# Two norms at the seam of two blocks made one, column tiles alternated, pooling and weight loads reordered

## The reference, cut to what matters

```
h = concatenate([meta_tokens, x], axis=1)
for l in range(2):
    u = rms_norm(h, norm_w[l]) @ w_in[l]
    f_in, f_gate, p_in, p_gate, c_q, c_kv, k_r, a_gate = split(u)
    y_f = fourier_mix(f_in, fourier_w[l])        # DFT over tokens and over 64 channels
    y_p = pool_mix(p_in, pool_w[l], pool_scale)  # window means over 2, 4, 8, 16 tokens
    y_a = mla_mix(c_q, c_kv, k_r, ...)
    h = h + concatenate([y_f * silu(f_gate), y_p * silu(p_gate), y_a * silu(a_gate)]) @ w_out[l]
return rms_norm(h, final_norm_w)[:, 16:]
```

## Time and profile before

| | us |
|---|---|
| median of 3 runs | 4046.81 (4042.68 to 4050.09) |
| the profiled execution | 4042.67 |
| its span | 4040.9 |
| mean granted clock of TensorE | 0.964 of 2.4 GHz |

### The profile page before, as it was taken

The page is one execution under the profiler, slowest core; times in us unless marked ns, Lnnn a source line. Parts: engine busy times, 40 slices in busy tenths (PEclk is TensorE's granted clock), DMA queues, the critical chain, the costliest instruction groups (busy, mean ns, idle before and its releaser), DMA issues.

```text
span 4040.9 us, 51127 instructions
## 1 busy us (share of the span) xinstructions
PE 3743.9 (93%) x20820; PEld 3311.2 (82%) x20820; DVE 1718.9 (43%) x3136; ACT 1265.5 (31%) x2868; POOL 1091.6 (27%) x806
## 2 busy tenths in 40 slices
PE   6999998999999899999899999968988998898898
PEld 5787777888887788777778888858988998898898
DVE  6624554433325552455443332554334334333333
ACT  3212443034331211244313333122245422134541
POOL 2533222321113362322231221326310023530002
PEclk9999999999999999999999999979989999998999
DMA  3111110401114212111130112322100031110012
GB/s 113 37 68 63 35 50 32 147 31 42 42 40 176 87 42 78 47 40 44 42 141 29 42 40 79 130 83 65 43 26 19 20 108 56 60 52 13 14 41 95
DMA packets 85195, 243.91 MB, mean 60 GB/s; under 512 B 10720, under 2 KB 25312, under 8 KB 84960
## 3 DMA queue, kind: packets, MB, share of 16 engines
q1 hardware_dynamic: 84960, 240.64, 17.4%
HBM read 190.07 MB, written 50.53 MB: 60 GB/s over the span
## 4 chain that ended last, share of the span: by engine, by line
PE 70%; DVE 14%; ACT 7%; issue 5%; DMA 2%; POOL 2%; SPq 1%; DVEq 0%; POOLq 0%; ACTq 0%
PE pj L1212 27%; PE pS L1212 21%; PE po L1420 4%; PE po L1311 4%; PE pS L1400 3%; PE pS L1402 2%; DVE tmp L2030 1%; PE pS L1282 1%; DVE KK L2042 1%; PE pS L1283 1%; PE pt L1298 1%; DVE tmp L2033 1%; ACT PT L1612 1%; PE pj L1386 1%; DVE tmp L2027 1%
## 5 line engine op out<-in xcount | busy, mean ns | idle before, releaser
L2471 POOL TENSOR_SCALAR Whi<-stage 128x1024 fp32r<-128x1024 f32 (+4 forms) x272 | 277.8, 1021 | 2138.9 <-DMA stage<-wstream 1328.4
L1212 PE MATMUL pj<-Hhi,Whi 128*128 128x512 f32 x1648 | 657.5, 399 | 8.3 <-DVE Hlo L1901 3.3
L1212 PE MATMUL pj<-Hhi,Wlo 128*128 128x512 f32 x1648 | 645.5, 392 | 0.0
L1212 PE MATMUL pj<-Hlo,Whi 128*128 128x512 f32 x1648 | 645.0, 391 | 0.0
L2473 POOL TENSOR_TENSOR Wlo<-stage,Whi 128x1024 fp32r<-128x1024 f32 (+4 forms) x272 | 621.9, 2287 | 22.7
L1212 PEld LDWEIGHTS pj<-Hhi,Whi 128*128 128x128 f32 x1648 | 311.6, 189 | 76.3 <-ACT PT L1612 6.6
L1212 PEld LDWEIGHTS pj<-Hhi,Wlo 128*128 128x128 f32 x1648 | 311.0, 189 | 66.8
L1212 PEld LDWEIGHTS pj<-Hlo,Whi 128*128 128x128 f32 x1648 | 311.6, 189 | 61.4
L1212 PE MATMUL pS<-Hhi,Whi 128*128 128x512 f32 x784 | 312.7, 399 | 12.2 <-DVE Hlo L1901 5.1
L1212 PE MATMUL pS<-Hlo,Whi 128*128 128x512 f32 x784 | 310.0, 395 | 0.0
L1212 PE MATMUL pS<-Hhi,Wlo 128*128 128x512 f32 x784 | 309.5, 395 | 0.0
(11 more groups left out here) (389 smaller groups left out, 7735.8 us busy)
## 6 DMA issues: line engine op xcount, KB each, us to landing
stage<-wstream SPq DMA_DIRECT2D x228, 512.0 KB, 4.3
merged<-Mb SPq DMA_DIRECT2D x32, 512.0 KB, 2.9
Mb<-merged SPq DMA_DIRECT2D x32, 512.0 KB, 5.1
gates<-tmp SPq DMA_DIRECT2D x48, 256.0 KB, 2.2
TH<-gates SPq DMA_DIRECT2D x24, 512.0 KB, 6.1
xres<-X SPq DMA_DIRECT2D x16, 520.0 KB, 5.7
xr<-xres SPq DMA_DIRECT2D x16, 520.0 KB, 4.6
X<-xT SPq DMA_DIRECT2D x16, 256.0 KB, 6.8
```

What stands on the lines that cost most here:

```text
L1212: x = pe.e.matmul(ps, w[a][:, v.koff + k * P:v.koff + k * P + P], moving(v.of, b, k, v.t0, v.n), start=k == 0 and i == 0, stop=k == v.K - ...
L2471: pool.e.tensor_scalar(upper, stage, 1.0, 0.0, ALU.mult, ALU.add).then_inc(*pool.tick("whi", c))
```

## The change

1. **The seam.** While the last projections of block 1 run, ACT also squares x times final_g (`square` of kind "g", into accg) and DVE adds those. With s = sum(x^2) and g = sum((x final_g)^2), the two norms in one are x final_g norm_w / sqrt(g/D + EPS (s/D + EPS)): `last_sums` makes that per half of the tokens, with the meta tokens' squares in one more column. `row_spread` spreads it, `norm2` scales X directly with the product of the two gains (vec 98 to 105, and vec 60 to 67 for the 16 meta tokens). `between` is gone. The residual needs X by the first norm still: `scaled` does this on DVE behind `amix` in layer 0, and `scaled_out` stores it behind the DFT. The meta tokens and the rope tables come at the start of the last `output1` (`tables2_in`).
2. **Column tiles.** In both layers f0, f1 and p0 alternate by k in all three column tiles, and the norm of tile c + 1 stands in the order ahead of the group of tile c. `phase()` and `small_in` move behind the three groups.
3. **Weight loads.** Load c stands at the unit behind the last use of weight c - 3.
4. **Split by ACT.** For five of the eight DFT pieces ACT makes the upper half and POOL the lower one only.
5. **Pooling.** `pool0` moves behind the DFT, the window sums of `pool1` (`pool1_sums`) directly behind it, and the rest of `pool1` between the gates of p0 and those of f1. The order of the gates is f0, p0, f1, p1, and was f0, f1, p0, p1.
6. Tiles get other addresses in SBUF, and `ones` shrinks to 8 columns.

```diff
-        loaded = 0
-        for u, upto in self.upto:
-            last = min(upto, len(self.weights) - 1)
-            u["loads"] = range(loaded, last + 1)
-            loaded = max(loaded, last + 1)
+        at = 0
+        for c in range(len(self.weights)):
+            at = max(at, self.first[c].id if c < NR else self.used_at[c - NR] + 1)
+            self.units[at].setdefault("loads", []).append(c)
...
     def between(self, sums):
-        ph = self.phase()
-        rs = self.spread(sums) + self.spread(self.rstd("1", [self.accs[1]], D, 1))
-        u = self.put("between", rs=[("rs", x.id) for x in rs], x_ready=self.x_ready[0] + self.x_ready[1])
-        self.accs = {0: ("accs", u.id)}
-        self.phase()
-        u = self.put("between_out", of=u.id)
+        power = ("power", sums.id, 0)
+        self.rs = [self.row_spread("RS2", 0, [(24, META)] + [(20 + i, P) for i in range(3)], power)]
...
     def fourier_pool(self, l, norm):
+        f = [self.in2("f_copy", key("f", i), x=i, box={}, emptied="f_copy") for i in range(2)]
+        p = [self.in2("p_copy", key("p", i), x=i, box={}, emptied="p_copy") for i in range(2)]
+        for c in range(3):
+            if c < 2:
+                norm(c + 1)
+            self.together([f[0][c], f[1][c], p[0][c]], {} if c else self.inside)
+        f_ready = [("f_copy", f[i][2].id) for i in range(2)]
+        self.phase()
...
         self.put("small_in", l=l)
-        self.together([f[0][0], f[1][0], p[0][0]], self.inside)
-        for c in (1, 2):
-            self.run([f[0][c], f[1][c], p[0][c]])
         u = self.put("gmix", l=l, po_free=self.po_free)
...
-        u = self.put("pool0", l=l, p_ready=p_ready[0], folded=("lo", fold, 5), a_ready=a_ready)
-        z_ready = [("lo", u.id, 1)]
+        if l == 0:
+            self.put("scaled", rs=("rs", row[1].id))
+            lv_free = ("final1", 7)
...
+        if l == 0:
+            self.put("scaled_out")
+        u = self.put("pool0", l=l, p_ready=p_ready[0], folded=("lo", fold, 5), lv_free=lv_free, a_ready=a_ready)
+        z_ready = [("lo", u.id, 1)]
+        levels = self.put("pool1_sums", l=l, p_ready=p_ready[1], z_ready=z_ready)
...
-        for i in range(2):
+        def gate_f(i):
             self.run(self.in2("gate_f", key("fg", i), x=i, box={}, sets=slot, emptied="silu2", fy_ready=fy_ready[i], ph3=ph3,
                               y_free=self.y_free, l=l))
...
+        gate_f(0)
         gate_p(0, z_ready)
-        u = self.put("pool1", l=l, p_ready=p_ready[1], z_ready=z_ready, z_free=z_free[0], a_ready=a_ready)
+        u = self.put("pool1", l=l, levels=levels.id, z_free=z_free[0], a_ready=a_ready)
+        gate_f(1)
         gate_p(1, [("lo", u.id, 1)])
...
+def by_act(key):
+    return key[0] == "dft" and key[1:] not in ((0, 0, 0), (0, 0, 1), (1, 0, 0))
...
+    def last_sums(u):        # TensorE
+        for i, acc in enumerate((m.acc, m.accg)):
+            for j in range(4):
+                t0, col = 512 * u.c + j * P, 16 * u.c + 4 * i + j
+                x = pe.e.matmul(m.po[:, col:col + 1], acc[:, t0:t0 + P], ones[:, 0:1], start=True, stop=True)
+        if u.c == 0:
+            pe.wait_ge(("meta_square", u.meta))
+            for k in range(8):
+                x = pe.e.matmul(m.po[0:META, 8:9], m.sqm[:, k, :], ones[:, 0:1], start=k == 0, stop=k == 7)
...
+    def split(c):            # ACT, at the unit that carries load c
+        act.wait_ge(("w_in", c))
+        act.wait_ge(("wused", c - NR))
+        act.e.activation(m.W[c % NR][0][:, 0:n], m.stage[c % NS][:, 0:n], ACT.Copy).then_inc(*act.tick("whi_act", c))
...
+    def pool1_sums(u):       # POOL
         pool.wait_ge(u.p_ready)
         for x in u.z_ready:
             pool.wait_ge(x)
```

More of the change, by code:

```diff
@@ L189, in memory @@
[L189 to L195, removed]
@@ L328, in add @@
         if u.opens:
-            u.box["c"] = self.weight(u, u.key, u.ahead)
+            u.box["c"] = self.weight(u.key)
         if u.box is not None:
             u["c"] = u.box["c"]
+            if u.ends:
+                self.used_at[u.c] = u.id
         if u.banked:
@@ L798, in output1 @@
                     if i == 0:
-                        sums = self.rstd("1", [self.accs[0]], D, 0, within=True)
+                        sums = self.last_sums(0, meta.id) if last else self.rstd("1", [self.accs[0]], D, 0, within=True)
                     else:
-                        u["inside"] = {3: [sums]}
+                        u["inside"] = {4 if last else 3: [sums]}
             ring_free[e % 2] = ("residual", u.id)
@@ L877, in fourier_pool @@
         self.run(p[1])
+        row = self.scaled(self.half_sums, fold) if l == 0 else []
         p_ready = [("p_copy", p[i][2].id) for i in range(2)]
@@ L1241, in spread, with row_spread @@
         x.then_inc(*pe.tick("spread", u.id))
+    def row_spread(u):
+        pe.wait_ge(u.powers)
+        pe.wait_ge(u.free)
+        o = 0
+        for col, n in u.cols:
+            x = pe.e.matmul(m.pj[u.bank][:, o:o + n], m.st[0:n, col:col + 1].to_broadcast([n, P]), ident[0:n, 0:n],
+                            start=True, stop=True)
+            o += n
+        x.then_inc(*pe.tick("row_spread", u.id))
+    def last_sums(u):
+        for x in u.accs:
+            pe.wait_ge(x)
+        pe.wait_ge(u.po_free)
+        for i, acc in enumerate((m.acc, m.accg)):
[6 more added lines that the diff above has]
+                x = pe.e.matmul(m.po[0:META, 8:9], m.sqm[:, k, :], ones[:, 0:1], start=k == 0, stop=k == 7)
+        x.then_inc(*pe.tick("last_sums", u.id))
     def ln(u):
@@ L1469, in square, with meta_squares, row_spread @@
         dst = acc[:, u.t0:u.t0 + u.n] if u.k == 0 else sq[u.slot][:, 0:u.n]
-        act.e.activation(dst, src, ACT.Square).then_inc(*act.tick("square", u.id))
+        if u.of == "g":
+            act.e.activation(dst, src, ACT.Square, scale=m.vec[:, 52 + u.k:53 + u.k]).then_inc(*act.tick("square", u.id))
+        else:
+            act.e.activation(dst, src, ACT.Square).then_inc(*act.tick("square", u.id))
+    def meta_squares(u):
+        for k in range(8):
+            act.wait_ge(("meta_in", k))
+        phase_met(u)
+        act.e.activation(m.sqm[:, :, :], m.X[:, :, 0:META], ACT.Square).then_inc(*act.tick("meta_square", u.id))
+    def row_spread(u):
+        n = sum(x for _, x in u.cols)
+        act.wait_ge(("row_spread", u.id))
+        act.wait_ge(u.freed)
+        phase_met(u)
+        act.e.activation((m.RS2 if u.dst == "RS2" else m.RSy)[:, u.t0:u.t0 + n], m.pj[u.bank][:, 0:n], ACT.Copy).then_inc(
+            *act.tick("rs", u.id))
     def spread(u):
@@ L1839, in scalar_program @@
     for u in order.units:
+        for c in u.loads or ():
+            if by_act(order.weights[c]):
+                split(c)
         if u.kind in parts:
@@ L2470, in load @@
         pool.wait_ge(("wused", c - NR))
-        pool.e.tensor_scalar(upper, stage, 1.0, 0.0, ALU.mult, ALU.add).then_inc(*pool.tick("whi", c))
-        pool.wait_ge(("whi", c))
+        if by_act(order.weights[c]):
+            pool.wait_ge(("whi_act", c))
+        else:
+            pool.e.tensor_scalar(upper, stage, 1.0, 0.0, ALU.mult, ALU.add).then_inc(*pool.tick("whi", c))
+            pool.wait_ge(("whi", c))
         TT(lower, stage, upper.bitcast(F32), ALU.subtract).then_inc(*pool.tick("wlo", c))
@@ L2566, in pool1 @@
         level(u, 3, m.lv[1], m.lv[0], 4, 4, 8, 1048)
-    parts = {"phase": phase, "sums": sums, "norm": norm, "mix_in": mix_in, "ln": ln, "values": values, "between": between,
-             "proj": proj, "small_in": small_in, "pool0": pool0, "pool1": pool1}
+    parts = {"phase": phase, "sums": sums, "last_sums": last_sums, "norm": norm, "mix_in": mix_in, "ln": ln, "values": values,
+             "proj": proj, "small_in": small_in, "pool0": pool0, "pool1_sums": pool1_sums}
     for u in order.units:
```

241 lines of the change are left out of this document (136 added, 105 removed).

## The result

The changed kernel takes **4126.6 us** (median of 4 runs, 4117.4 to 4128.6), the kernel before in the same runs 4045.8: a ratio of 1.0195, with a 95% interval of 1.0177 to 1.0212. It is 1.95% slower. I had forecast 4037 and a range of 4005 to 4061. The profiled execution took 4128.6 (span 4126.6), so it is compared with the one before of 4042.7.

The account below looks back on a forecast made before the run. TensorE, busy 93% of the span, was taken as the bound, so only its gaps and slow clock counted. Terms -40 + 31 - 12 - 3.5 + 11.5 + 3 = -10 took the median 4046.8 to 4037 us, range 4005 to 4061.

Parts of the forecast that it names:

- part 6: Attention a: splits now ahead of a step's power delay it, mostly covered; +3 us, bounds 0 to +36.
- Rival (c): Attention a: ACT stands behind each delayed power, so the next step's copies and exponentials come late; +31, 4068 us; chance 0.17.
- The seam: Between the blocks: one norm for two and an earlier third weight shorten TensorE's waits; -40 us, bounds -32 to -43.
- The small inputs: Before gmix in both layers: TensorE waits for small transfers issued behind POOL's splits; +31 us, bounds 0 to +36.
- Loads one slot later: Layer starts and layer 1's copy stall: two third-weight waits and the stall vanish; -12 us, bounds -6 to -14.
- DFT: ACT's five upper halves delay odd copies but ready later weights: layer 0 +1 us, layer 1 -4.5.
- the 14.2 us by the rule on the two engines: Layer 0's DFT: scalings plus all lower halves, if DVE and POOL lock each other out; sum 1.5 us higher.
- Pooling: Both layers: POOL's levels delay the first Fy product, so TensorE waits for gate banks; +11.5 us, bounds -15 to +20.
- (a): Before gmix: the small inputs don't hold TensorE, so part of +31 shrinks to nothing; 4006 us; chance 0.18.
- (b): Pooling: POOL clears its levels before TensorE's banks fill, so its term becomes -15; 4011 us; chance 0.12.
- (d): Between the blocks: the seam yields only 30, with a late third weight and longer slow clock; 4047 us; chance 0.08.
- The row behind the prediction: Profile row of DVE scalings: two grew by 2.2 us beside one 3.4 us POOL add, agreeing with the lock in kind.

Follow-up runs that it names:

- e4: Changed kernel with only a weight's transfer issued earlier, ahead of the gate store; POOL still splits before the power: 4088.6 us, ratio 1.0105.
- e8: Changed kernel with POOL's powers put ahead of loads, plus square buffers alternating in order of making, as before: 4058.9 us, ratio 1.0030.
- e2: Kernel before with only the weight-load rule changed, to one slot after the last use of the weight three back: 4129.5 us, ratio 1.0206.
- e1: Changed kernel with the old rule for weight loads, weight c loaded when weight c-2 is opened: 4048.1 us, ratio 1.0004.
- c3: c1 with the loads in the last merge of each layer of block 1 back on the old rule: 4028.3 us, ratio 0.9975.
- e5: Changed kernel with POOL's powers ahead of loads, plus POOL's mark before its splits and small inputs issued before the third transfer: 4047.4 us, ratio 1.0006.
- e7: Changed kernel with POOL's powers ahead of loads, plus pool1_sums behind the first three gate_f tiles: 4057.5 us, ratio 1.0031.
- d1: c3 with the seventh DFT piece's split back on POOL and the seam's last two squares behind the norm's first two slices: 4026.4 us, ratio 0.9954.
- c1: Changed kernel with four edits together: powers before loads, small inputs first, pool1_sums later, square buffers alternating: 4034.4 us, ratio 0.9982.

## Why the prediction was wrong

**The step that failed is part 6.** It reads: "a 3.6 us split delays the power by 1.8 us. The next use of its result is at 413.15, 5 us after it is ready, so it is mostly covered", +3, bounds 0 to +36. It measured +64. Two things in it were wrong. First, I let the split start "as the filler ends". A split starts when its weight has landed, and the request stands right behind the weight's last use, on SP behind the gate store: it lands 5 us after that. At five loads of layer 0 POOL waited for a transfer, 54.7 us in all, with a power queued behind four of them. In the kernel before the transfer of the load shown was as late (issued at 423.35, landed 4.9 us later) and harmless, since POOL did the power first:

```profile
424.53 0.55 POOL L2514 TENSOR_TENSOR st<-st,vec 128x1 f32<-128x1 f32 x1 [8.33 <-DVE st L2173]
...
428.33 1.06 POOL L2471 TENSOR_SCALAR Whi<-stage 128x1024 fp32r<-128x1024 f32 x1 [2.98 <-DMA stage<-wstream]
```

That is the 38 us of e4. Second, the cover. I took 5 us of slack from one step early in a head and gave it to all. Ten steps of each layer had a split ahead of the power, 20 and not 40 in all; e4 gives 26 us for them by the splits alone. Rival (c) had named place and mechanism and its +31 is near that part, but it too left the transfer out. It had a chance of 0.17.

**Left out altogether:** the diff changes a buffer index for the squares, and I gave it no term. In the first sums the squares of one half of x share one buffer, so ACT and DVE take turns, 1.45 us a square: the first sums start 4.4 us earlier in e8. The rest of the 9.3 us at the start goes with the load rule: at 340 us e2, with the rule and the old index, is 2.7 us behind the kernel before, and e1, with the old rule and the new index, 5.4. In the rest of block 2 the rule and the index make 8.8 us more, of which e1 leaves 1.1. In the rest of block 1 the ends of the two merges lose 3.9 and 3.4 us, where a split now falls beside DVE's last work; c3 shortens TensorE's waits there from 4.6 to 2.2 and 2.3.

**The seam, -32.9 for -40.** The mechanism was right. Two terms were small. In times of before (after, less the delay of 74.1) the projection ends at 2650.4 and not at 2648.5, since the sums for both norms take 2.3 us and the granted clock behind them is 0.60 until the projection ends, and one addition behind it took 2.75 us for 0.69; and the nine tiles took 42.5 us at a granted clock of 0.87 where I had 38.8: slow clock cost 5.5, not 3.

**The small inputs, +30.6 for +31,** by the chain as told: three splits for POOL (7.3 us), then 4.5 us from first issue to first use. e5 undoes it and confirms the cause.

**Loads one slot later, -8.8 for -12.** The copy stall in layer 1 is gone as told (-5.3). The two waits for a third weight are gone too, but the wait for the norm ahead of each grew: from 3.3 to 5.4 us at the start of block 1's layer 1 and from 2.7 to 4.8 in block 2's. So they gave 2.9 and 0.6 us, forecast 4.5 and 2.5.

**DFT, +0.2 for -3.5.** ACT's odd copies come 3.2 us later (5.5 for 2.3 in layer 1), not 1.8: the gain at the weight behind is spent. In layer 0 the eight scalings took 13.3 us, forecast 13. The +1 for layer 0 doesn't follow from its own terms either: 1.8 + 0.7 - 2.6 is about nothing, before any slow clock. And the 14.2 us by the rule on the two engines are 1.2 above 13, not 1.5.

**Pooling, +10.4 for +11.5,** by the queue on POOL that I named; in e7, where the queue is gone, so is the wait of 7.0 us, though shorter waits take most of its place.

So rivals (a), (b) and (d) didn't happen, though the seam came near (d). All parts but attention a and the two without a term make +4 together (forecast: -13); those three make 82.

## What to carry to other kernels

When a rule moves loads in an in-order queue, look at each unit that the load is moved past, and price the wait for its transfer before the work of the load: a request and its consumer need not move together. Cover read at one step holds for that step; count in how many steps the moved work stands ahead of what another engine waits for. Read index arithmetic of buffers in a diff for every caller: a formula that alternates in one loop order is constant in another.

## What the hardware showed

**DVE and POOL lock each other out.** An addition of 512 columns from two SBUF tiles takes 0.69 us alone; beside a lower half on POOL, at the last residual of the changed kernel:

```profile
2725.86 2.34 POOL L2580 TENSOR_TENSOR Wlo<-stage,Whi 128x1024 fp32r<-128x1024 f32 x1
...
2726.00 2.75 DVE L1972 TENSOR_TENSOR acc<-acc,sq 128x512 f32<-128x512 f32 x1 [0.70 <-ACT sq L1556]
```

It ends 0.55 us after POOL does. The changed kernel's trace has 17 additions of this shape that start while a lower half runs, with 1.3 to 2.3 us of it left: all 17 end 0.55 us after it, while those that meet none take 0.68 or 0.69. So the time goes by POOL's end and not by a shared rate, and d1's scaling of 16 columns shows the same. That is the exclusive lock which the Trainium skill tells of (page SBUF — State Buffer, section "SBUF: two separate sides"), and here the trace agrees. The row behind the prediction, too, fits better than I said: of the two scalings there one took 1.28 us and the other 3.40, and it ended 1.08 us after POOL's add. In the DFT the rule's sum (14.2) was no better than mine (13), since 13.3 us were measured. A rule for loads thus also decides beside which work of DVE a split falls: at the end of the last merge, where it is two subtractions, that is 2.4 us in layer 0 (c1 against c3).

**A power on POOL is dear for its size, and goes with its columns:** 0.55 us for one, 0.85 for three, 1.02 for four, 1.65 for eight and 1.81 for nine, the others in the changed kernel's trace (three more of four columns took 1.45 there).
